# Attention of the first block: v for all heads ahead of the heads, two projections a step, and the SSM's scans and outputs at new places

## What is computed

```python
n = rmsnorm(h, g_mix)
z = n @ w_in                       # 1024 x (3*1536 + 512 + 2048)
q, k, v = ...                      # 12 heads of 128, three groups of 4 heads
u = z[..., o1:o1 + SSM_WIDTH]      # 512 channels for the SSM
gate_attn, gate_ssm = ...          # 2 x 1024, through a sigmoid
for gi, (window, dilation) in enumerate(((128, 1), (512, 4), (2048, 16))):
    o_g, l_g = dilated_band_attention(q[hs], k[hs], v[hs], dilation, window // dilation)
wts = softmax(stack(lses)); attn = sum(wts * outs)
...
ar, ai, bu_re, bu_im -> lax.associative_scan(...)   # complex diagonal state, 32 groups of 64
y = C h + D u
```

## Time and profile before

| what | us |
|---|---|
| runs shown | 1785.03, 1785.89, 1787.0; median 1785.89 |
| profiled execution: its own time | 1786.5 |
| span of its instructions | 1784.7 |
| PE busy | 1772.2 (99%) |
| DVE busy | 1042.7 (58%) |
| ACT busy | 786.2 (44%) |
| POOL busy | 266.7 (15%) |

### The profile page before, as it was taken

One profiled execution on the slowest core, in us unless ns is written; L12 is line 12 of the kernel. 1 busy time (PEld: TensorE's weight loads), 2 busy tenths in 40 slices (PEclk: granted clock), 3 DMA queues, 4 the chain that ended last, 5 costly groups with the idle time before them and its releaser, 6 DMA issues.

```text
span 1784.7 us, 20965 instructions
## 1 busy us (share of the span) xinstructions
PE 1772.2 (99%) x8086; PEld 1419.8 (80%) x8086; DVE 1042.7 (58%) x1675; ACT 786.2 (44%) x1248; POOL 266.7 (15%) x349
## 2 busy tenths in 40 slices
PE   9999999999999999999999999999999999999998
PEld 7788888878887888888887678777778788888887
DVE  8865554765566545554479796256544765435543
ACT  6554454524344221222264666356653453223343
POOL 4676536300000000000001110322210000000000
PEclk9999999999999999999999999999999999999999
DMA  5322223134344545555341422421143232233222
GB/s 206 108 89 89 71 89 92 47 118 154 94 139 153 188 146 176 208 189 176 119 130 46 149 83 83 142 72 60 36 156 104 91 96 93 89 96 94 93 93 71
DMA packets 65411, 202.06 MB, mean 113 GB/s; under 512 B 7520, under 2 KB 11872, under 8 KB 65312
## 3 DMA queue, kind: packets, MB, share of 16 engines
q1 hardware_dynamic: 65312, 200.72, 34.2%
HBM read 192.30 MB, written 8.40 MB: 112 GB/s over the span
## 4 chain that ended last, share of the span: by engine, by line
PE 95%; DVE 2%; ACT 1%; issue 0%; DMA 0%; SPq 0%; ACTq 0%; DVEq 0%
PE bank L258 29%; PE bank L260 28%; PE bank L259 28%; PE bank L660 2%; PE bank L688 1%; PE bank L673 1%; PE bank L304 1%; PE bank L356 1%; PE bank L341 1%; PE bank L537 1%; DVE wlo L1445 1%; PE bank L386 0%; PE bank L377 0%; PE bank L300 0%; PE bank L277 0%
## 5 line engine op out<-in xcount | busy, mean ns | idle before, releaser
L258 PE MATMUL bank<-tiler,whi 128*128 128x512 f32 x2260 | 911.7, 403 | 1.9 <-DVE tiler L1529 0.9
L260 PE MATMUL bank<-tiler,wlo 128*128 128x512 f32 x2260 | 892.6, 395 | 0.0
L259 PE MATMUL bank<-tiler,whi 128*128 128x512 f32 x2260 | 892.1, 395 | 0.0
L854 ACT ACTIVATE whi<-raw 128x1024 fp32r<-128x1024 f32 x284 | 298.8, 1054 | 518.1 <-PE bank L260 508.9
L258 PEld LDWEIGHTS bank<-tiler,whi 128*128 128x128 f32 x2260 | 425.8, 188 | 114.9 <-issue 14.6
L260 PEld LDWEIGHTS bank<-tiler,wlo 128*128 128x128 f32 x2260 | 425.5, 188 | 100.2
L259 PEld LDWEIGHTS bank<-tiler,whi 128*128 128x128 f32 x2260 | 426.0, 189 | 97.4 <-issue 1.4
L1445 DVE TENSOR_TENSOR wlo<-raw,whi 128x1024 fp32r<-128x1024 f32 x263 | 326.6, 1246 | 262.7 <-ACT whi L854 262.3
L2292 POOL TENSOR_TENSOR stat<-stat,scl 128x4 f32<-128x4 f32 x7 | 7.5, 1074 | 745.9 <-DVE stat L1965 428.2
L2231 DVE SCALAR_TENSOR_TENSOR tile<-bank,sm,tile 128x511 f32<-128x511 f32 x42 | 31.5, 749 | 87.3 <-ACT tile L1407 43.8
L2283 POOL TENSOR_TENSOR wlo<-raw,whi 128x1024 fp32r<-128x1024 f32 x21 | 50.1, 2384 | 207.2 <-ACT whi L854 207.2
(11 more groups left out here) (385 smaller groups left out, 1570.6 us busy)
## 6 DMA issues: line engine op xcount, KB each, us to landing
raw<-wst SPq DMA_DIRECT2D x284, 512.0 KB, 3.7
wide<-wadaT SPq DMA_DIRECT2D x52, 512.0 KB, 3.5
tile<-xT SPq DMA_DIRECT2D x16, 256.0 KB, 6.0
spare<-tile SPq DMA_DIRECT2D x16, 256.0 KB, 2.2
tile<-spare SPq DMA_DIRECT2D x16, 256.0 KB, 5.8
out<-tile SPq DMA_DIRECT2D x8, 256.0 KB, 2.5
tile<-gblk SPq DMA_DIRECT2D x5, 256.0 KB, 4.6
us<-tile SPq DMA_DIRECT2D x4, 256.0 KB, 2.3
```

What stands on the lines that cost most here:

```text
L258: e.matmul(bank, whi[:, o:o + 128], hi, start=start, stop=False)
L259: e.matmul(bank, whi[:, o:o + 128], lo, start=False, stop=False)
L260: e.matmul(bank, wlo[:, o:o + 128], hi, start=False, stop=stop).then_inc(*sig("blk", n))
L854: e.activation(whi[:, c % NHL * W:(c % NHL + 1) * W], raw[:, c % NRAW * W:(c % NRAW + 1) * W], ACT.Copy).then_inc(*sig("hi", c))
```

## The change

- v is projected for all heads of a group together, by tokens: `group_v(g)` takes a block of 128 tokens as the stationary operand and streams 512 columns of weights (four heads). For groups 1 and 2 the token block is every fourth token (`token_block`). The result needs no transpose; four copies a group (`v_copies`) bring it to `O[g][0]`, widened to four tiles, which later holds the outputs too. All three groups come before step 1; they take 12 chunks.
- Group 2 is sorted by 4 residues like group 1, with a mask of k % 4 == q % 4.
- Steps 1 to 11 hold two projections, q and k. `score(b)` stands at the end of part 0, `values` of the head before at the sixth block of the next step's part 0, in bank 4.
- The SSM's rounds start at a = 1, 5, 9 and 12. The scans come in phase 2, behind `top` and one `wlo`, ahead of `rope`. `ssm_c` comes at the end of part 0 of steps 4, 8, 12 and 15.
- `rope(0)` stands behind a chunk's `wlo`; `decay`, `inputs` and `step_powers` lie between chunks of v.
- `rows` come one projection later each; `table4` is split over three turns; SP's thresholds follow.

```diff
-WIDE = {CP: 3, CR: 2, WADA[0]: 2, WADA[1]: 2, WADA[2]: 2, PM: 5}
+WIDE = {O[0][0]: 4, O[1][0]: 4, O[2][0]: 4, CP: 3, CR: 2, WADA[0]: 2, WADA[1]: 2, WADA[2]: 2, PM: 5}
-DIL = (1, 4, 16)
+DIL = (1, 4, 4)
+        def ssm_step(a):
+            for j, s in enumerate((1, 5, 9, 12)):
+                if 0 <= a - s < 3:
+                    return j, a - s
+            return 0, None
...
+            def token_block(tile, g, n):
+                if g == 0:
+                    return R(tile)[:, n * 128:(n + 1) * 128]
+                return R(tile).rearrange("p (l r) -> p r l", r=4)[:, n, :]
...
+                        e.matmul(bank, token_block(hi, g, n), whi[:, o:o + 512], start=k == 0, stop=False)
+                        e.matmul(bank, token_block(lo, g, n), whi[:, o:o + 512], start=False, stop=False)
+                        e.matmul(bank, token_block(hi, g, n), wlo[:, o:o + 512], start=False, stop=k == 7).then_inc(
+                            *sig("blk", n0 + n))
...
-                            turn(B[4], VT[b % 2], 4, "vtr", b)
...
+                    proj("in", m, bank, N1, range(3, 6))
+                    if part == 0 and 2 <= a <= 13:
+                        values(a - 2)
+                    proj("in", m, bank, N1, range(6, 8))
                     if part == 0:
...
+                        if phase == 0:
+                            ssm_turn(j)
+                        if phase == 1:
+                            ssm_direct(j)
+                        if a in (4, 8, 12, 15):
+                            ssm_c((4, 8, 12, 15).index(a))
...
-                    if a == 13 and part < 2:
+                    if a == 13 and part:
                         for g in range(3):
-                            rows(part, g)
-                    if 8 <= s - 36 <= 11:
-                        share(s - 44)
+                            rows(part - 1, g)
+                    if a >= 12 and 8 <= t <= 11:
+                        share(t - 8)
...
+            for i in range(12):
+                prep(first.get(("in", 24), 0) + CB * i)
+                if i == 0:
+                    rope(0)
+                if i == 3:
+                    decay()
+                if i == 5:
+                    inputs()
+                if i == 7:
+                    step_powers()
...
+                if att:
+                    top(b, 0)
+                    if b % 3 == 0:
+                        top(b, 1)
                 if a < 12:
                     start_of("in", 12 + m0)
                 else:
                     start_of("in", 41 + 3 * (a - 12))
...
+                if phase == 2:
+                    ssm_scan(j)
...
-                if phase == 1:
-                    ssm_scan(j)
...
-                    if m == 1:
-                        table4()
+                    if 1 <= m <= 3:
+                        table4(m - 1)
...
-    consts[:, 384:512] = np.where((k <= q) & (k // 32 == q // 32), f(0), neg)
+    consts[:, 384:512] = np.where((k <= q) & (k % 4 == q % 4), f(0), neg)
```

## The result

The changed kernel takes 1799.15 us (median of four runs, 1795.1 to 1800.49), the kernel before, beside it, 1785.59. The ratio is 1.0071, with a 95% interval of 1.0059 to 1.0084: slower, by 12.7 us by this ratio and by 13.6 between the medians. The prediction had the sign, but said +4.3 us and a range up to 1796.0; the measured time lies above it. The runs further down were made in three groups, each on a chip of its own with the kernel before beside it; their ratios are to that one.

What follows compares the result with a forecast made beforehand. TensorE (PE), busy 99% of the span, was taken as the bound. -9.0 + 0 + 4.8 + 8.5 = +4.3 us on 1786.5 gave 1790.8; with the median of the runs 0.6 lower, the forecast was 1790.2 us, range 1781.5 to 1796.

Steps and rivals of the forecast that it cites:

- The low clock: TensorE, after the long wait at `ssm_c(3)`, restarts at a lower clock: +2.7 us, near 1793; a rival, chance 0.13.
- The strided block: Stationary read every fourth element in 192 v matmuls: taken at 0; as a rival +2 to +17 us, chance 0.08.
- The gains: 48 v transposes gone 5.3 us, waits for first rope and exponentials 3.2, `table4` wait 0.5: 9.0 us less.
- the last scan: Fourth scan behind `weights()` in step 14: PE waits 5.4 to 9.7 us, mostly at `ssm_c(3)`; 8.5 taken.
- The steps after v: Rope beside `ssm_out` slows POOL, so PE waits 1.7, 1.2 and 2.0 us at `ssm_c` (steps 4, 8, 12): +4.8.
- R: The end of the second `rows` on PE, from which the times of the fourth scan's chain were counted.

## Why the prediction was wrong, step by step

Between +4.3 and +12.5 us lie 8.2. The low clock, which the sum had at 0, is 4.0 of them, and the contention of rope and `ssm_out` 1.7 (6.5 in place of 4.8, at another wait than the one forecast). The strided block is 1.4, the spacing of the projections about 1, and about 1 is unexplained. The gains and the last scan came out 0.5 and 0.4 better.

**The gains** were right: 9.0 forecast, 9.5 found.

**The clock** is the step that cost most. I held the 8.5 us wait likely, put the low clock behind it at nothing in the sum and called it a rival of 0.13. But the one follows from the other once the wait is there: after 7.7 us it fell in five of five profiled executions, so the case had nearly the chance of the wait itself. The size, 2.7 us, was near the 2.5 found at `ssm_c(3)`. The page of the Trainium skill that I named, "TensorE: Matmul & The Clock Gate", section "What's actually happening", agrees with the trace, 0.50 granted from 364.5 to 374.5 us. A second fall, 1.5 us behind a wait of 2.8 us for a rope, was in no case of mine.

**"The steps after v"** failed too, in which engine is late. That the rope would run beside `ssm_out`, both at a reduced rate, was right. But I charged the whole slowdown to POOL, at 2.0 + 0.85 us, and kept DVE's rope at the 4.05 us of the earlier trace rows. I called those rows the same pair of instructions; they show the rope beside POOL products of 128 x 128, and here they are 128 x 508. In fact POOL needed 8.8 to 9.1 us instead of 7.7, not 10.5, and the rope's four products 6.5. So POOL's state was in time at `ssm_c`, and the rope was late at `score`, which stands ahead of `ssm_c` in PE's order. That 4.8 us (by its own three terms 4.9) lies near 6.5 is partly luck: the forecast waits, at `ssm_c`, were 0. I had worked out a budget for the chain that ends in `ssm_c` and none for the rope's own. It takes two lines, once the rope's length is known: the k copy ends 0.26 + 1.1 us after the k projection, the rope 7.3 us later, together 8.7; PE has the turn, a projection and the values, 0.45 + 5.6 + 0.9 = 7.0. That is 1.7 us of wait, and 1.76 was found. The text named waits for the ropes of steps 2, 8 and 11 as a way to be wrong; they came for those of steps 3, 7, 8 and 11, so two of the four had been named, without a price.

**"The last scan"** stood: 8.5 forecast, 8.1 found, at the place given, with `weights()` ending 17 us behind R as worked out. Putting that scan back does not gain all of it: `ssm_out(3)` has to be done before `relative()` starts.

**The strided block** was taken at 0 and costs 1.4 us, within the 0 to 2 us that I gave as the smaller of two prices. The Trainium skill's "SBUF — State Buffer", section "Door 1: The DMA port swizzle", which speaks of a penalty for such a stream, is borne out by the count of 76 and 77 matmuls against 79 in 18 us; the page gives no size, and the measured one is 3% of a matmul.

**The range.** Its upper end did take the costs together, at 4.8 + 9.7 + 2.7 + 2 - 9.0 = +10.2 us. The profiled execution came out 2.3 above that: the ropes 1.7 and the second low clock 1.3 more than the highest price given, spacing and the unexplained rest 2, against 2.7 less at the last scan, the stride and the gains. So even the range had no room for a second fall of the clock, nor for a change of spacing.

## What to carry to other kernels

When work is moved so that two engines with heavy elementwise streams run side by side, budget both of them at the slowed rate, and check every consumer of either in the order in which the bounding engine meets them. A wait of some us (here 2.8 and more) on a TensorE that is otherwise always busy can have a second price behind it; count it in the same case as the wait. An instruction that fits into DVE's idle time is worth trying right behind its operands: here moving the scans by about one projection turned +12.7 us into -4.9, and eight independent transposes in front of the late scores made it -8, part of which is spacing.

## What the runs showed of the hardware

- **DVE and POOL together.** POOL's product of 128x508: 1.28 us alone, 1.6 to 2.0 beside the rope, 2.1 to 2.3 beside a `wlo`. DVE's 64x512: 0.68 alone, 1.4 to 1.8 beside POOL; 32x512: 0.68 alone, 1.6 to 2.0. DVE's 4x512 went from 0.68 to 1.49 and 1.66, so the slowdown came with rows of 4 partitions too. Why two such streams slow each other was not tried.
- **The clock behind a wait.** After waits of up to 1.8 us of PE it stayed at 1.00 in every trace. After 2.8 us at `score` it fell in four of the six profiled executions that had this wait and stayed up in two. After 2.8 us at `share(0)` it fell in both, after 7.7 us in all five. It was back 3 to 7 us after work had begun again. Of executions without a trace only the mean clock is known; in kernels without a long wait some have 0.999, and one 0.998, so falls elsewhere cannot be excluded for them.
- **Two spacings of the same matmuls.** In long undisturbed stretches the projections follow each other every 232.4 or every 233.3 ns, at a granted clock of 1.00 both times, and one kernel's stretches hold the one or the other. The table by stretches, of the kernel before and of the changed one:

```profile
600.00:900.00 300.00, 300.00 (x1293) 1.00 0.48 166
1450.00:1750.00 300.00, 300.00 (x1287) 1.00 0.30 93
```

```profile
600.00:900.00 300.00, 300.00 (x1288) 1.00 0.48 169
1450.00:1750.00 300.00, 300.00 (x1292) 1.00 0.31 95
```

0.4% is 2.3 us over 580 us. The last 6000 matmuls, about three quarters of the time and the same in every version of the changed kernel, took 1356.6 us in one profiled execution and 1360.2 in others. The spread of the runs of one kernel (1783.3 to 1788.3 for the one with all four scans moved) is of that size, so differences of 2 or 3 us between versions here rest on the traces and not on the times. What chooses between the two stays open, it was not tried. About 1 us of the account above is also unexplained.
